# Delta-rule levels: the late modulation's products stand between a level's two products

## What is computed

```
c_act = silu(c)
mod = c_act @ w_ada[layer] + b_ada[layer]      # layer 0, layer 1
mkv = c_act @ w_ada_kv + b_ada_kv
```

```
L = where(strict, (k_beta @ k.T) * decay, 0)
sol = triangular_solve(L + I, rhs, lower=True, unit_diagonal=True)
attn = where(tril, (q @ k.T) * decay, 0)
```

## Time and profile before

| what | value |
| --- | --- |
| median of three runs | 1159.59 us (1159.42 to 1159.63) |
| the profiled execution, its own time | 1159.38 us |
| its span | 1157.6 us |
| TensorE busy | 1114.9 us, 96% of the span |
| VectorE, ScalarE, GpSimd busy | 516.1, 514.7, 371.1 us |
| chain that ended last: TensorE's share | 83% |
| head pairs, levels and W | 247.14 to 345.38 us |

### The profile page before, as it was taken

How to read it: one execution, slowest core, us unless ns; L and a number is a source line. 1 busy time by engine, 2 the same in 40 slices (tenths; PEclk the granted TensorE clock), 3 DMA queues, 4 the chain that set the end, 5 groups by cost and what they waited for, 6 DMA issues and landing times.

```text
span 1157.6 us, 20420 instructions
## 1 busy us (share of the span) xinstructions
PE 1114.9 (96%) x8466; PEld 879.9 (76%) x8466; DVE 516.1 (45%) x938; ACT 514.7 (44%) x907; POOL 371.1 (32%) x148
## 2 busy tenths in 40 slices
PE   5999999989999999999999999999999999999998
PEld 3688886767768889777776668888877777678767
DVE  4575553455543366242234882853013332331562
ACT  5223226753335534453365883433335434753530
POOL 0134342232246341434334001333343213433260
PEclk7999999999999999999999999999999999999999
DMA  9822331276751132234522101322232322224201
GB/s 315 261 69 83 109 100 46 73 256 210 231 185 38 38 109 64 83 98 139 128 73 73 38 1 37 109 86 79 91 102 59 107 80 72 75 79 156 97 1 73
DMA packets 103004, 119.32 MB, mean 103 GB/s; under 512 B 4679, under 2 KB 89207, under 8 KB 102791
## 3 DMA queue, kind: packets, MB, share of 16 engines
q1 hardware_dynamic: 99054, 115.08, 31.4%
q10 hardware_dynamic: 3864, 3.01, 0.9%
HBM read 110.75 MB, written 2.10 MB: 97 GB/s over the span
## 4 chain that ended last, share of the span: by engine, by line
PE 83%; ACT 6%; DVE 5%; issue 3%; DMA 1%; ACTq 1%; SPq 0%; POOL 0%; DVEq 0%
PE ps L2079 43%; PE ps L2876 4%; PE ps L2125 2%; PE ps L2472 2%; PE ps L2686 2%; PE ps L2721 2%; PE ps L2498 2%; PE ps L2163 1%; PE ps L2704 1%; PE ps L2220 1%; PE ps L2243 1%; PE ps L2296 1%; PE ps L2842 1%; PE ps L2829 1%; DMA ada_a<-in_w_ada_dram 1%
## 5 line engine op out<-in xcount | busy, mean ns | idle before, releaser
L615 POOL TENSOR_TENSOR wlo<-raw,whi 128x2048 fp32r<-128x2048 f32 x53 | 245.3, 4629 | 525.6 <-ACT whi L781 513.1
L781 ACT ACTIVATE whi<-raw 128x2048 fp32r<-128x2048 f32 x52 | 99.3, 1912 | 191.7 <-PE ps L2079 152.6
L621 POOL TENSOR_TENSOR wlo<-raw,whi 128x2048 fp32r<-128x2048 f32 x10 | 46.4, 4639 | 112.0 <-ACT whi L870 63.5
L1809 DVE TENSOR_TENSOR_SCAN taken<-kept,taken 128x255 f32<-128x255 f32 (+2 forms) x64 | 51.2, 852 | 21.4 <-ACT taken L1200 21.4
L1290 ACT ACTIVATE p<-sc,nmx 128x256 f32<-128x256 f32 x64 | 32.0, 501 | 45.9 <-PE ps L2829 44.7
L1906 DVE CUSTOM_DVE_ANT_0 sc<-ps,biast 128x256 f32<-128x256 f32 (+1 forms) x64 | 22.4, 393 | 65.7 <-PE ps L2818 36.8
L870 ACT ACTIVATE whi<-raw 128x2048 fp32r<-128x2048 f32 x11 | 21.1, 1917 | 63.2 <-PE ps L2079 63.2
L2079 PE MATMUL ps<-hC_hi,whi 128*128 128x512 f32 x184 | 47.0, 397 | 0.8 <-POOL wlo L615 0.8
L2079 PE MATMUL ps<-hC_lo,whi 128*128 128x512 f32 x184 | 45.5, 390 | 0.0
L2079 PE MATMUL ps<-hC_hi,wlo 128*128 128x512 f32 x184 | 45.4, 389 | 0.0
L2079 PEld LDWEIGHTS ps<-hC_hi,whi 128*128 128x128 f32 x184 | 33.7, 188 | 14.8 <-issue 6.4
(11 more groups left out here) (504 smaller groups left out, 2641.9 us busy)
## 6 DMA issues: line engine op xcount, KB each, us to landing
raw<-in_w_in_dram SPq DMA_DIRECT2D x24, 1024.0 KB, 5.1
raw<-in_w_in_a_dram SPq DMA_DIRECT2D x16, 1024.0 KB, 5.6
raw<-in_w_ada_dram SPq DMA_DIRECT2D x8, 1024.0 KB, 5.1
late_w<-in_w_ada_dram SPq DMA_DIRECT2D x8, 1024.0 KB, 5.7
raw<-in_w_kv_dram SPq DMA_DIRECT2D x8, 1024.0 KB, 5.2
raw<-in_w_in_b_dram SPq DMA_DIRECT2D x8, 1024.0 KB, 6.0
ada_a<-in_w_ada_dram SPq DMA_DIRECT2D x4, 1024.0 KB, 10.2
ada_b<-in_w_ada_dram SPq DMA_DIRECT2D x4, 1024.0 KB, 12.9
```

The source lines that it names most:

```text
L615: pool.tensor_tensor(wlo[:, s, :], raw[:, s, :], whi[:, s, :].bitcast(F32), ALU.subtract).then_inc(lo_ready, 1)
L621: pool.tensor_tensor(wlo[:, s, :], raw[:, s, :], whi[:, s, :].bitcast(F32), ALU.subtract).then_inc(lo_ready, 1)
L781: A(whi[:, s, :], raw[:, s, :], ACT.Copy).then_inc(hi_ready, 1)
L1809: last = dve.tensor_tensor_scan(taken[:, r % 3, keys], kept[:, r % 3, keys], taken[:, r % 3, keys], 0.0, ALU.mult, ALU.add)
```

## The change

In levels 0 to 2 of the first three pairs one half is made between the first and the second products, behind the preparation of the next heads, where there was none; in all other levels three halves are made there, where there was one. Behind the second products nothing is made in levels 0 to 3, where there were two halves (levels 0 to 2 of the first three pairs) or one; in level 4 two are made, as before.

```
@@ -2480,8 +2480,7 @@
                             keys_keys(h)
                         for h in (nxt, nxt + 1):
                             keys_queries(h)
-                    else:
-                        filler(1)
+                    filler(1 if nxt is not None and lv < 3 else 3)
                     if lv == 0:
                         if p:
                             pe.wait_ge(w_evac, 2 * p)
@@ -2498,7 +2497,8 @@
                             last = mm(block64(X_BANKS[s], 0, i, n), yib[side(n), (p + lv) % 2, 4 * s + i, :],
                                       XT[side(n), 2 * p + s, i, :], start=True, stop=True)
                         last.then_inc(xn_full, 1)
-                    filler(2 if lv == 4 or nxt is not None and lv < 3 else 1)
+                    if lv == 4:
+                        filler(2)
```

## The result

The changed kernel takes 1170.92 us, median of four runs (1169.18 to 1173.99), where the kernel before took 1159.51 us in the same comparison: 1.0097 times as long, 95% interval 1.0081 to 1.0113. The forecast was 1165.3 us, with a range up to 1168. The side was right, the size was half of what came. The profiled execution took 1169.18 us, 9.8 us more than the one of before; of these, 9.2 us lie between level 0's first products of the first pair and the last second products of the last pair: 94.60 us before, 103.83 after. It is the fastest of the four; the median lies 1.7 us above it, and no profile shows what the others spent that on. I call these 94.60 or 103.83 us the stage; A and B are a level's first and second products, as in the prediction.

A forecast was written before the change was run, and what follows sets the result against it. TensorE's own instruction stream was taken to bound the four head pairs. 4.2 us for the order of halves plus 1.7 for a late load made +5.9, so 1165.3 us; range 1162 to 1168 held some 0.8.

The forecast's parts named there:

- the loads: SP's queue, third into last pair: four weight loads issued in bursts, the last landing about 1.7 us late.
- The late load: Last pair, level 1: TensorE waits about 1.7 us between A and B for a load; bounds nothing and 3 us.
- the prediction's own sign: In the first three pairs and the last: longer pairs without a DMA wait would mean the first rival holds.
- first rival: Last pair: the last load isn't late, so only +4.2 us, 1163.7 us in all; chance 0.22.
- The order: First three pairs: moving the halves costs +1.39 us in each, +4.2 us in all.
- the very chain named: B of level 1 to A of level 3: ScalarE's K copies, queries' products, VectorE's inverse and turned tile; gain 0.57 us.
- Level 3 to level 4: First three pairs, A to A: VectorE's work doesn't depend on the halves' place; interval stays 4.18 us, cost 0.
- The last pair: Fourth head pair: joined halves save what bare second products give back; 13.94 us before, 13.93 after, cost 0.
- GpSimd's later start: Last pair: GpSimd's gated products and decayed state come 0.9 us later; cost taken as 0, bounds 0 and 0.9.
- worse than the sum: Rival: two or more loads late, or ScalarE and VectorE slip at each level; over +8.5, 1168 and more; chance 0.05.
- Faster: Rival: level 3's three 0.81 us waits get covered and bare B-to-A intervals fill with ready work; about 1156.7 us; chance 0.06.
- the heads' chain doesn't own the levels: Rival, levels 0 and 1: line 2426 comes right behind TensorE's own work; 1159.4 us, or up to 1161; chance 0.09.

The follow-up runs named there:

- after_small: The changed kernel with the late modulation's loads from the fifth unit on cut to their first eighth; 1162.41 us, ratio 1.0021.
- before_restore_late: The kernel before with GpSimd's reset of yib for the next pair's level 0 held until level 4's second products; 1158.61 us, ratio 0.9995.
- after_hold_out: The changed kernel with SP holding two loads of the next stage's weights until the last pair's level 1 second products; 1173.98 us, ratio 1.0108.
- before_thin0: The kernel before with two halves behind level 0's second products, first three pairs, cut from four matmuls to one each; 1162.64 us, ratio 1.0014.

## Why the prediction was right and wrong

*The term that was missing.* "Sum: 4.2 + 1.7" has no term for TensorE's own instructions. The step that failed is **the loads**: it worked out that four loads are issued within 7 us and asked only whether their data come in time. It did not ask what else goes through the same DMA engines. The kernel before had the sign of it, 0.8 us of "issue" in the waits of this stage, in the middle of line 2472's products, and I left that row out. It became 4.9 us, and behind the longest gap the clock fell for 3.4 us, 1.7 us more. By the stages this closes. Without its one wait of 0.67 us after_small has 96.36 us, so the loads cost the changed kernel 103.83 - 96.36 = 7.5 us, the half clock included. They cost the kernel before 94.60 - 93.52 = 1.1. The difference, 6.4 us, and the order's own 96.36 - 93.52 = 2.8 are the 9.2 us of the profile. The rows of waits give 5.8 in place of the 6.4, (4.9 - 0.8) + 1.7, as they count each wait some 0.2 short.

*The late load,* 1.7 us: did not show. By the prediction's own sign, longer pairs and no wait for a DMA, its first rival would hold, but that one had 1163.7 us. The load came 1.9 us behind the time at which the order alone would have wanted it (339.9 against 338.0), so bunching and landing were right, but TensorE was later still. Its place in the sum was taken by what the same burst does to the fetches.

*The order,* forecast 4.2 us: 2.9 by the pairs of the two kernels with small loads. By intervals, second pair, after_small against before: level 0 A to B +0.57 (forecast 0.55); B of level 0 to line 2426 5.01 for 5.06 (0); B of level 0 to B of level 1 +0.50 (0.55); B of level 1 to A of level 3 -0.58 (-0.57), by the very chain named; level 4 to the next pair +0.86 (0.86). **Level 3 to level 4** was the one that missed: -0.40 where I had 0. I had called VectorE's work there independent of where the halves stand. It isn't: the later B moves GpSimd's reset off VectorE's copy. Three times 0.40 is 1.2 of the 1.3 us between 4.2 and 2.9.

*The last pair:* forecast 13.93 us after for 13.94 before; 14.69 and 14.04 with small loads, all of the 0.65 between them being the wait within a group. So the order costs nothing there, as forecast. *GpSimd's later start:* forecast 0, with 0.9 as the bound: from the last B to the end the two profiles take 815.83 and 816.29 us.

*The rivals:* "worse than the sum" had the side and 1 in 20, with "two or more loads late" as its mechanism, which is not what happened. "Faster" and "the heads' chain doesn't own the levels" are refuted by the 5.01 us that stayed.

## What to carry to other kernels

Where a stage is one engine's instruction stream, loads that are issued in bursts can cost twice, by their own lateness and by what they hold up: count what is queued on the DMA engines when the stream's next instructions are fetched, above all where the matmuls are small and 270 instructions last only a few microseconds. "Issue" waits in the middle of a group of like instructions were the mark of it here, and one in the profile before the change said that the reserve there was used up. Look at the granted clock too before a difference in time is put down to an edit: in eight of these thirteen kernels it fell in the stage or behind it (the last microseconds of the span left out). And filler work belongs behind the product whose consumer chain is longest: placed behind the wait that this chain ends in, it is paid in full.

## What was not expected of the hardware

- With two or more 1 MB loads under way, four fetches of TensorE's instructions started 2.9 to 3.2 us late, and one at the start of the stage 4.3; with one load under way at a time, 1.8 at most. The waits that they made stood at the same instructions in both profiles of the changed kernel. Some of these fetches waited for more than the load that was being moved, and none for all that was queued.
- The granted clock fell to 0.50 for 3.4 us behind one idle gap of TensorE: of 1.89 us, ended at 339.72 in the changed kernel, although it was busy 3.95 of the 4 us from 333 on, and of 1.81 us, ended at 331.15 in before_restore_late. Behind the gaps of 1.50 and 1.51 us of the changed kernel it did not. In after_hold_out it fell behind one of 1.77 us (280.61) and not behind another (335.81).
- A masked copy on VectorE took 0.84 us in place of 0.45 where a copy of GpSimd had begun 0.07 us before it.
- Two halves of one matmul each (two records) took TensorE 0.98 us in before_thin0 (278.38 to 279.36), where two whole ones of four matmuls take 1.00.
